# The expert weights move in 2 MB and in 8 KB pieces, and the row order follows

## The reference

```
def expert_step(acc, ep):
    w1, b1, w2, b2, g = ep                       # (1024, 2048), (2048,), (1024, 1024), (1024,)
    hdn = x @ w1 + b1
    gt = jnp.minimum(hdn[:, :D_FF], SWIGLU_LIMIT)
    up = jnp.clip(hdn[:, D_FF:], -SWIGLU_LIMIT, SWIGLU_LIMIT)
    act = (up + 1.0) * gt * jax.nn.sigmoid(SWIGLU_ALPHA * gt)
    return acc + g[:, None] * (act @ w2 + b2), None
```

## Time and profile before

| what | value |
|---|---|
| time, median of 3 runs | 1397.82 us (1396.66 to 1398.46) |
| span of the profiled execution | 1394.0 us |
| the profiled execution's own time | not among the times shown; the median lies 3.8 us above its span |
| TensorE busy | 1257.9 us, 90% |
| DVE, ACT, POOL busy | 373.9, 182.2, 98.6 us |
| mean granted TensorE clock | 0.951 |
| read from HBM | 436.65 MB |

### The profile page before, as it was taken

How to read it: one execution, slowest core, us unless ns; L and a number is a source line. 1 busy time by engine, 2 the same in 40 slices (tenths; PEclk the granted TensorE clock), 3 DMA queues, 4 the chain that set the end, 5 groups by cost and what they waited for, 6 DMA issues and landing times.

```text
span 1394.0 us, 15526 instructions
## 1 busy us (share of the span) xinstructions
PE 1257.9 (90%) x5839; PEld 604.8 (43%) x5839; DVE 373.9 (27%) x700; ACT 182.2 (13%) x338; POOL 98.6 (7%) x214
## 2 busy tenths in 40 slices
PE   4988898899999999898999999999999899989885
PEld 3645576343434343443434343434344443434254
DVE  6899514121111112121211111111122121120122
ACT  2113403001101010101010110101010101010022
POOL 4565200000000000000000000000000000000000
PEclk8997999899999999999999999999999999998988
DMA  9331213789999999999999999999999999998600
GB/s 313 108 126 60 77 56 129 296 328 407 394 388 386 403 378 397 384 401 377 398 364 383 393 381 400 386 397 379 402 371 406 384 393 377 374 364 347 240 1 32
DMA packets 89134, 438.45 MB, mean 315 GB/s; under 512 B 13616, under 2 KB 16816, under 8 KB 55264
## 3 DMA queue, kind: packets, MB, share of 16 engines
q1 hardware_dynamic: 88528, 437.60, 78.4%
q10 hardware_dynamic: 576, 0.45, 0.1%
HBM read 436.65 MB, written 2.41 MB: 315 GB/s over the span
## 4 chain that ended last, share of the span: by engine, by line
PE 85%; DVE 9%; issue 3%; ACT 2%; DMA 0%; ACTq 0%; DVEq 0%; SPq 0%
PE ps L907 37%; PE ps L923 17%; PE ps L893 10%; PE ps L863 6%; PE ps L797 2%; PE ps L1033 2%; PE ps L914 2%; PE ps L511 2%; PE ps L866 1%; PE ps L591 1%; DVE region L1683 1%; DVE region L1686 1%; DVE region L1680 1%; PE ps L556 1%; PE ps L976 1%
## 5 line engine op out<-in xcount | busy, mean ns | idle before, releaser
L907 PE MATMUL ps<-ring_up,region 128*64 128x512 f32 x2112 | 461.8, 595 | 2.9 <-issue 1.6
L907 PEld LDWEIGHTS ps<-ring_up,region 128*64 128x64 f32 x2112 | 163.4, 137 | 283.3 <-issue 281.4
L923 PE MATMUL ps<-ring_dn,region 128*64 128x512 f32 x1056 | 240.3, 608 | 12.4 <-issue 11.0
L1679 DVE TENSOR_SCALAR region<-ps 128x512 f32<-128x512 f32 x33 | 22.8, 692 | 701.6 <-PE ps L907 701.6
L923 PEld LDWEIGHTS ps<-ring_dn,region 128*64 128x64 f32 x1056 | 82.3, 140 | 157.1 <-issue 155.0
L893 PE MATMUL ps<-region,n_tok 128*128 128x128 f32 (+1 forms) x768 | 136.1, 307 | 0.0
L893 PEld LDWEIGHTS ps<-region,n_tok 128*128 128x128 f32 (+1 forms) x768 | 104.2, 187 | 41.2 <-issue 12.2
L1222 ACT ACTIVATE region<-region 128x512 f32<-128x512 f32 x33 | 20.8, 629 | 499.7 <-DVE region L1679 499.7
L863 PE MATMUL ps<-region 128*128 128x512 f32 (+1 forms) x136 | 80.2, 744 | 2.6 <-issue 1.3
L478 POOL COPY region<-kst 128x64 f32 (+1 forms) x33 | 7.8, 238 | 1040.6 <-PE ps L907 1040.6
L1234 ACT ACTIVATE region<-ps 64x512 f32<-64x512 f32 x66 | 39.1, 592 | 320.7 <-PE ps L923 320.3
(11 more groups left out here) (354 smaller groups left out, 888.2 us busy)
## 6 DMA issues: line engine op xcount, KB each, us to landing
ring_up<-in_w_up_dram SPq DMA_DIRECT2D x264, 1024.0 KB, 11.2
ring_dn<-in_w_down_dram SPq DMA_DIRECT2D x132, 1024.0 KB, 7.0
ring_up<-in_w_in_dram SPq DMA_DIRECT2D x4, 1280.0 KB, 9.9
ring_dn<-in_w_out_dram SPq DMA_DIRECT2D x1, 4096.0 KB, 26.3
ring_up<-in_w_ple_gate_dram SPq DMA_DIRECT2D x4, 1024.0 KB, 6.4
x_tok<-in_x_prompt_dram SPq DMA_DIRECT2D x2, 512.0 KB
ring_up<-in_w_glu_dram SPq DMA_DIRECT2D x1, 1024.0 KB, 16.2
region<-in_w_ple_proj_dram SPq DMA_DIRECT2D x1, 1024.0 KB
```

What stands on the lines that cost most here:

```text
L907: m = mm(ps[64 * (q % 2):64 * (q % 2) + 64, q // 2, :], xe[:, k, slots] if k < UP else one_hot, w, start=(k == 0), stop=(k == UP))
L923: m = mm(ps[64 * half:64 * half + 64, O_B, :], act_t[:, f % 4, 64 * (f // 4):64 * (f // 4) + 64], ring_dn[:, f, 512 * half:512 * half + 51 ...
L1679: V.tensor_scalar(g_lim, bank(0), LIMIT, None, ALU.min).then_inc(Z["g_rdy"], 1)
```

## The change

`w_up` moves in four transfers of 2 MB an expert where there were eight of 1 MB; a partition now receives 16 KB that are contiguous in HBM, two neighbouring rows of the matrix. `w_down` still moves in four transfers of 1 MB, but a partition receives two neighbouring rows (8 KB contiguous) where it received two rows that lie 128 apart (4 KB each). So slot `k` of a ring holds other rows of the matrix than before: of each 256 rows, the even or the odd ones. To match, the gather and the transposes of the activation take every second column of a 256-column piece as their stationary operand. The norm's weight is needed in the same order, so one more small load and two small transposes at the start put it into eight more columns of `vecs`. Number and size of all matmuls in the expert loop stay.

```diff
-UP, DN = 8, 4
+UP, DN = 4, 4
...
-            up_w = A["w_up"][0].rearrange("e (k p) n -> e k p n", p=P)
-            dn_w = A["w_down"][0].rearrange("e (s k p) n -> e s p k n", p=P, k=2)
+            up_w = A["w_up"][0].rearrange("e (s p k) n -> e s p k n", p=P, k=2)
+            dn_w = A["w_down"][0].rearrange("e (s p k) n -> e s p k n", p=P, k=2)
...
-                    if first and k == 5:
+                    if first and k == 2:
                         embedding_loads()
                     if first:
-                        sp.wait_ge(*((Z["q_ps"], 6) if k < 5 else (Z["glu_ps"], KM) if k == 5 else (Z["s5_free"], 1)))
+                        sp.wait_ge(*((Z["q_ps"], 6) if k < 2 else (Z["glu_ps"], KM) if k == 2 else (Z["s5_free"], 1)))
...
-                    sp.dma_start(ring_up[:, k], up_w[bass.ds(e, 1), k].rearrange("e p n -> (e p) n")
+                    sp.dma_start(ring_up[:, 2 * k:2 * k + 2], up_w[bass.ds(e, 1), k].rearrange("e p k n -> (e p) k n")
...
-                sp.wait_ge(Z["up_free"], (n + (NE - 1)) * UP + (k + 1))
+                sp.wait_ge(Z["up_free"], (n + (NE - 1)) * UP + (k // 2 + 1))
...
-            pe.wait_ge(ld_vec, 16 * 7)
-            tr(bank(7, V_N), rows[0:V_N, 0:P], ident[0:V_N, 0:V_N]).then_inc(Z["vec_ps"], 1)
+            pe.wait_ge(ld_vec, 16 * 8)
+            tr(bank(7, V_ROW), rows[0:V_ROW, 0:P], ident[0:V_ROW, 0:V_ROW])
+            in_pairs = rows[64:68, 0:2 * P].rearrange("s (n k) -> s k n", k=2)
+            for k in range(2):
+                m = tr(ps[:, 7, V_ROW:V_ROW + 8].rearrange("p (s k) -> p k s", k=2)[:, k], in_pairs[:, k], ident[64:68, 64:68])
+            m.then_inc(Z["vec_ps"], 1)
...
+            n_by_row = n_tok[:].rearrange("p c (s n k) -> p c s k n", s=4, k=2)
...
-                        m = mm(ps[:, X_B[k // 4], (k % 4) * P:(k % 4 + 1) * P], n_tok[0:nt, c, k * P:(k + 1) * P],
+                        m = mm(ps[:, X_B[k // 4], (k % 4) * P:(k % 4 + 1) * P], n_by_row[0:nt, c, k // 2, k % 2],
...
+                by_row = act_v.rearrange("p (s n k) -> p s k n", s=2, k=2)
                 for j in range(4):
-                    m = tr(ps[:, T_B, j * P:(j + 1) * P], act_v[:, j * P:(j + 1) * P], ident)
+                    m = tr(ps[:, T_B, j * P:(j + 1) * P], by_row[:, j // 2, j % 2], ident)
...
+            act.dma_start(rows[64:68, 0:2 * P], A["norm_ffn"][0].rearrange("(s n) -> s n", s=4)).then_inc(ld_vec, 16)
```

More of the change, by code:

```diff
@@ L64 @@
 K_N = K_OF + 4
-V_MIX, V_FFN, V_PLE, V_OUT, V_D, V_GLU, V_N = 0, 8, 16, 24, 32, 36, 40
+V_MIX, V_FFN, V_PLE, V_OUT, V_D, V_GLU, V_ROW, V_N = 0, 8, 16, 24, 32, 36, 40, 48
 AT_KVTOK, AT_SCORES, AT_VALUES, AT_TURN = 6, (6, 9), (8, 12), (11, 15)
@@ L121, in hybrid_layer @@
         ps = ctx.enter_context(nc.psum_tensor("ps", [P, 8, 512], F32))
-        ring_up = sb("ring_up", [P, UP, 2 * FF])
+        ring_up = sb("ring_up", [P, 2 * UP, 2 * FF])
         ring_dn = sb("ring_dn", [P, 2 * DN, D])
@@ L898, in up @@
             def up(t, slots):
[L900 to L903, removed]
+                for k in range(KD + 1):
+                    if k == KD:
                         pe.wait_ge(Z["hot_rdy"], t + 2)
+                    elif k % 2 == 0:
+                        pe.wait_ge(up_in[k // 2], 16 * t + 16)
                     for q in range(4):
[L906 to L909, removed]
+                        w = (ring_up[:, k] if k < KD else b_up)[:, q * 512:(q + 1) * 512]
+                        m = mm(ps[64 * (q % 2):64 * (q % 2) + 64, q // 2, :], xe[:, k, slots] if k < KD else one_hot, w,
+                               start=(k == 0), stop=(k == KD))
+                    if k == KD:
+                        m.then_inc(Z["hid_ps"], 1)
+                    elif k % 2 == 1:
+                        m.then_inc(Z["up_free"], 1)
             def turn_activations(t):
                 pe.wait_ge(Z["act_rdy"], t + 1)
+                by_row = act_v.rearrange("p (s n k) -> p s k n", s=2, k=2)
                 for j in range(4):
-                    m = tr(ps[:, T_B, j * P:(j + 1) * P], act_v[:, j * P:(j + 1) * P], ident)
+                    m = tr(ps[:, T_B, j * P:(j + 1) * P], by_row[:, j // 2, j % 2], ident)
                 m.then_inc(Z["at_ps"], 1)
@@ L975, in gather_visit @@
                     for c, (t0, nt) in enumerate(CHUNKS):
-                        m = mm(ps[:, 2, k * C:(k + 1) * C], n_tok[0:nt, c, k * P:(k + 1) * P], sel[0:nt, c, 0],
+                        m = mm(ps[:, 2, k * C:(k + 1) * C], n_by_row[0:nt, c, k // 2, k % 2], sel[0:nt, c, 0],
                                start=(c == 0), stop=(c == 2))
@@ L1658, in gathered @@
                     V.tensor_tensor(xe[:, 4 * h:4 * h + 4], ps[:, (2, 5)[h]].rearrange("p (k s) -> p k s", k=4),
[L1659 removed]
+                                    col(vecs[:, V_ROW + 4 * h:V_ROW + 4 * h + 4], 2 * C), ALU.mult
                                     ).then_inc(Z["xe_rdy"], 1)
@@ L1725, in gathered_visit @@
                 V.tensor_tensor(xe[:, :, 0:C], ps[:, 2].rearrange("p (k s) -> p k s", k=KD),
-                                col(vecs[:, V_FFN:V_FFN + KD], C), ALU.mult).then_inc(Z["xe_rdy"], 1)
+                                col(vecs[:, V_ROW:V_ROW + KD], C), ALU.mult).then_inc(Z["xe_rdy"], 1)
             def visit(v, e):
```

## The result

The changed kernel takes 1406.57 us (median of 4 runs, 1405.68 to 1411.93); the kernel before took 1397.66 in the same sitting (4 runs, 1396.66 to 1398.46). The ratio is 1.0073, 95% interval 1.0054 to 1.0092: slower by 8.9 us, three times what I had called the smallest difference that can be told.

What follows compares the result with a forecast made beforehand. The prediction took TensorE to bound the kernel, with no wait for a weight. Every part of the change summed to 0 us on the 1394.0 us span, giving a median of 1397.8 us, range 1394 to 1402, with 80% for no change.

Steps and rivals of the forecast that it cites:

- What bounds the kernel: Expert loop: TensorE is the bound, busy 90% of the span, and waits for no weight transfer despite full DMA engines.
- Transfers: Weight loads, 2 MB for `w_up` and 8 KB rows for `w_down`: 0 us, slowest 2 MB load landing in 18.3 us.
- first expert: Slot 4's load at the start now goes out with slot 5, still 67.8 us ahead of the first gather: 0 us.
- half the waits of `up`: TensorE's `up` has half the waits for weights; its records already stand back to back: 0 us.
- The start: One more small load and two small transposes, hidden under existing waits: 0 us, 0.4 us if that cover fails.
- Every second column as stationary operand: Stepped weight loads of TensorE in gather and transposes: taken as 0 us, bounded between 0 and 163 us.
- a gather above 8.6 us: Sign that would make the prediction wrong; a gather was expected to stay at 8.44 us.
- the DVE rows: Two DVE reductions used as evidence: 2.4 ns a word at a 128-byte step, 1.1 ns a word in a row.
- The upper bound of 163 us: Price if each stepped weight load of TensorE took twice its time: 135.2 + 9.5 + 18.7 us.
- Stepped loads are slower: Rival, 10%: stepped loads slow the gather, 9.5 us per 10 ns on a load; 1561 us at double time.
- The clock: TensorE's slow stretch after its wait costs 1.63 us a pair; it might give part of a small price back.
- fewer or more pairs: Rival, 4% faster, 1% slower: two pairs without the slow stretch give 1394.5 us, two more with it 1401.1.

Runs made afterwards that it cites:

- run 2: Changed kernel with its new loads, but gather and transposes read 128 columns in a row (products mismatched, same work): 1396.88 us, ratio 0.9998.
- run 5: Changed kernel, but DVE reads with the step and writes tokens and activation in the new order, so TensorE reads in a row: 1397.87 us, ratio 1.0007.
- run 3: Changed kernel's `w_up` loads and stepped gather, with `w_down` and transposes as in the kernel before: 1396.54 us, ratio 0.9996.
- run 4: Kernel before with only the changed kernel's `w_down` loads and stepped transposes: 1397.05 us, ratio 0.9996.
- run 6: Kernel before with the gather's first matmul done twice, all operands in a row: 1398.08 us, ratio 1.0009.
- run 7: Kernel before with the gather's first matmul done three times, all operands in a row: 1406.65 us, ratio 1.0065.
- run 8: Changed kernel with one of a gather's 24 matmuls left out: 1393.35 us, ratio 0.997 against the kernel before.
- run 10: Changed kernel with two of the three `combine` chunks moved into TensorE's wait for the activation: 1348.52 us, ratio 0.9661.
- run 12: Kernel before, its loads kept, with gather and transposes reading every fourth word (rows and weights mismatched): 1568.62 us, ratio 1.1225.

## Why the prediction was wrong

The forecast was no change, 1397.8 us in a range of 1394 to 1402; the kernel took 1406.57.

**What bounds the kernel** was right: TensorE, with no wait for a weight, in every run. **Transfers, first expert, half the waits of `up`** at 0 us were right (run 2, 0.9998), with landings of at most 14.7 us where I had allowed 18.3. **The start** was forecast at 0 to 0.4 us; the changed kernel's first pairs lie 1.1 us later, of which 0.3 lie ahead of the first gather, less than this point varies among the runs (237.2 to 239.9 us), and 0.4 in each of the two pairs behind it, as the stepped loads of a gather (8.56 us for 8.26 in the first) and of the transposes ask for.

**The step that failed** is "Every second column as stationary operand. ... I take 0". A stepped load is not free: 7 ns more in a gather, 67 ns more in the transposes at the high clock, 0.47 us in a pair, which the sum had at nothing. The sign that I had named for it, a gather above 8.6 us, came. My reason was a bound on the rate, 1.4 ns a word; it was taken from the pace of the gather, which tells how often a load takes a word when the words stand in a row and not what a step adds; and the DVE rows that I set beside it are of another engine, which run 5 shows to be indifferent to this step. The premise beside it was right, and is why 7 ns could matter: the loads set the gather's pace and nothing covers them. The runs show it: with loads of 189, 196 and 326 ns the gather spends 176, 182 and 319 ns on each. But the row that I gave for it was misread. The extra visit's gather of 9.47 us ran at the low clock from about 1277.7 us on; the 34 records that began at the high clock went out 155 ns apart, so half the columns did make it somewhat shorter. The upper bound of 163 us was far off the other way for a step of two. It is near what a step of four costs (171 us) by chance, as 110 us of those are the gathers and most of the rest is the clock.

The Trainium skill says in "SBUF — State Buffer", section "Door 1: The DMA port swizzle (why `[64,N]` ≈ `[32,N]`)", that two accesses to a 16-byte line are enough for full bandwidth. For DVE run 5 agrees (692 ns at a step of 8 bytes, 691 in a row). For TensorE's weight loads it doesn't hold: 141 ns became 209 in the transposes, and 189 became 196 in the gather. At one word a line the gather's loads rose to 326 ns, as the Trainium skill leads one to expect, but the transposes' stayed at 209 at the high clock, the same as with two words a line.

**The rival "Stepped loads are slower"** was what happened, and its point of decision, 3 ns on a load, was well placed. By its own price, 9.5 us for 10 ns, the gathers' 6.5 ns of pace (8.75 - 8.44 over 48) make 5.3 us and the transposes' 2.6 us, 7.9 in all; measured 8.9. That the two are so near is in part luck, since either half of this work alone cost nothing (runs 3 and 4). It had 10%, too little for an operation of which no row was at hand.

**The clock** was half right. I wrote that it might give a small price back; it does so fully for the added 0.10, 0.22 and 0.31 us a pair of runs 4, 6 and 3. That it takes more than the work at 0.45 and 0.47, as in run 7, I did not see. The case of "fewer or more pairs" with a slow stretch was the wrong picture: each of the 13 pairs has its slow stretch in either kernel, and in the changed one three of them last about twice as long.

What stays open: why a pair's length comes to rest at 64.85 us with up to 0.31 us of added work and is not held there when work is taken away (run 8), and why a step of two and one of four cost the same in the transposes and so differently in the gather.

## What to carry to other kernels

A new layout in HBM is paid for by whoever reads it from SBUF. Let the engine that has slack and doesn't mind the step (here DVE) make the order, so that TensorE's weight loads stay in a row, above all where loads and not matmuls set the pace. And ask first whether anyone waits for the transfer: larger transfers for DMA engines at 96% were worth nothing here, while a 2.8 us wait on TensorE, which also let its clock fall, was worth 4% of the time.

## What the runs showed of the hardware

- Weight loads of 128 columns of 32-bit words, at 2.4 GHz: 141, 209 and 209 ns at steps of one, two and four words in the transposes (at one and two words both behind a wait and behind a gather, at four behind a wait); 189, 196 and 326 ns in the back-to-back loads of a gather. At 1.2 GHz the transposes' loads take 227, 221 and 223 ns: there the step costs nothing.
- After a wait of 2.8 us in each pair TensorE ran for a stretch at 1.2 GHz, and the stretch ended at such a time that 0.31 us of added work left the pair at 64.85 us; 0.45 us made it 65.6 on average, with some stretches twice as long. Small gains or losses on TensorE between such waits can't be read from the total time.
- The wait is not the only thing that the clock falls after: it fell twice in 13 pairs behind a stop of 0.73 us that left it high in the other 11 (run 10), and in each pair within a gather of stepped loads, with no stop between it and the `up` ahead (run 12).
- In the loop DMA moved 415 GB/s with a share of 1.01 and PE waited for none of it.
